# Leaving out the unused 512-column products behind six closing norms and ahead of the RWKV mixer

## What is computed

```python
for layer in range(DEPTH_2):
    g = norm_g[layer]
    h = h + 0.5 * rms_norm_2(swiglu(rms_norm_2(h, g[0]), ffn_w_in[layer, 0], ffn_w_out[layer, 0]), g[1])
    u = rms_norm_2(h, g[2])
    ...   # m = RWKV-7 time mixing (layer 0) or windowed attention (layer 1)
    h = h + rms_norm_2(m, g[3])
    h = h + 0.5 * rms_norm_2(swiglu(rms_norm_2(h, g[4]), ffn_w_in[layer, 1], ffn_w_out[layer, 1]), g[5])
```

## Time and profile before

| | us |
|---|---|
| median of 3 runs | 2985.78 |
| the three runs | 2983.85, 2985.78, 2999.92 |
| the profiled execution | 2985.55 |
| its span, first to last instruction | 2983.8 |
| PE busy in the span | 2887.4 |
| POOL, DVE, ACT busy | 1359.9, 954.4, 948.8 |

### The profile page before, as it was taken

One profiled execution on the slowest core, in us unless ns is written; L12 is line 12 of the kernel. 1 busy time (PEld: TensorE's weight loads), 2 busy tenths in 40 slices (PEclk: granted clock), 3 DMA queues, 4 the chain that ended last, 5 costly groups with the idle time before them and its releaser, 6 DMA issues.

```text
span 2983.8 us, 46814 instructions
## 1 busy us (share of the span) xinstructions
PE 2887.4 (97%) x19364; PEld 2347.7 (79%) x19364; DVE 954.4 (32%) x1455; ACT 948.8 (32%) x1104; POOL 1359.9 (46%) x1111
## 2 busy tenths in 40 slices
PE   8999999999999998898999999999999999999998
PEld 7768778888888886677887788887888877788887
DVE  3441332223312126435553412125211246321213
ACT  3243232222322225643342322224222236422222
POOL 5454444444444454333433444444444457544444
PEclk9999999999999999999999999999999999999999
DMA  5202222222222221441201222222222220122222
GB/s 194 91 21 93 99 85 90 94 99 99 85 99 99 99 99 57 183 167 42 66 30 65 85 95 91 97 101 92 91 98 99 99 88 30 71 85 97 90 96 85
DMA packets 43423, 271.64 MB, mean 91 GB/s; under 512 B 4832, under 2 KB 4960, under 8 KB 13824
## 3 DMA queue, kind: packets, MB, share of 16 engines
q1 hardware_dynamic: 40032, 252.64, 23.7%
q10 hardware_dynamic: 3232, 16.65, 1.4%
HBM read 254.59 MB, written 14.68 MB: 90 GB/s over the span
## 4 chain that ended last, share of the span: by engine, by line
issue 44%; POOL 31%; PE 22%; DVE 2%; POOLq 0%; DVEq 0%; ACT 0%; DMA 0%; SPq 0%; ACTq 0%
POOL w_lo L551 29%; PE ps L875 6%; PE ps L694 3%; PE ps L695 3%; PE ps L696 3%; POOL ybuf L626 1%; PE ps L828 1%; PE ps L783 1%; PE ps L860 1%; POOL x_res L662 0%; PE ps L847 0%; PE ps L760 0%; DVE work L1713 0%; DVEq L1710 0%; PE ps L794 0%
## 5 line engine op out<-in xcount | busy, mean ns | idle before, releaser
L551 POOL TENSOR_TENSOR w_lo<-w_raw,w_hi 128x512 fp32r<-128x512 f32 x876 | 1117.4, 1307 | 1358.8 <-ACT w_hi L1194 1358.8
L694 PE MATMUL ps<-act_hi,w_hi 128*128 128x512 f32 x2240 | 881.8, 394 | 27.9 <-DVE act_lo L1655 15.8
L695 PE MATMUL ps<-act_lo,w_hi 128*128 128x512 f32 x2240 | 877.2, 392 | 0.0
L696 PE MATMUL ps<-act_hi,w_lo 128*128 128x512 f32 x2240 | 876.6, 391 | 0.0
L1194 ACT CAST w_hi<-w_raw 128x2048 fp32r<-128x2048 f32 x219 | 418.0, 1909 | 1013.0 <-PE ps L696 985.7
L694 PEld LDWEIGHTS ps<-act_hi,w_hi 128*128 128x128 f32 x2240 | 423.5, 189 | 129.9 <-issue 21.8
L696 PEld LDWEIGHTS ps<-act_hi,w_lo 128*128 128x128 f32 x2240 | 423.5, 189 | 88.9
L695 PEld LDWEIGHTS ps<-act_lo,w_hi 128*128 128x128 f32 x2240 | 423.8, 189 | 86.6
L694 PE MATMUL ps<-hid_hi,w_hi 128*128 128x512 f32 x1184 | 463.7, 392 | 9.0 <-POOL w_lo L551 8.1
L696 PE MATMUL ps<-hid_hi,w_lo 128*128 128x512 f32 x1184 | 461.9, 390 | 0.0
L695 PE MATMUL ps<-hid_lo,w_hi 128*128 128x512 f32 x1120 | 436.9, 390 | 0.0
(11 more groups left out here) (262 smaller groups left out, 2341.3 us busy)
## 6 DMA issues: line engine op xcount, KB each, us to landing
w_raw<-stream SPq DMA_DIRECT2D x223, 1024.0 KB, 4.8
spill<-work ACTq DMA_DIRECT2D x3, 2048.0 KB, 8.4
scratch<-spill SPq DMA_DIRECT2D x24, 256.0 KB, 4.2
work<-bias_in SPq DMA_DIRECT2D x1, 3072.0 KB, 17.5
work<-spill SPq DMA_DIRECT2D x12, 256.0 KB, 3.3
x_res<-x_in SPq DMA_DIRECT2D x4, 512.0 KB, 7.0
spill<-work ACTq DMA_DIRECT2D x2, 1024.0 KB, 4.9
spill<-area ACTq DMA_DIRECT2D x1, 2048.0 KB, 10.8
```

Source lines behind the costliest of these rows:

```text
L551: inst = tt(w_lo[:, s, a:a + 512], w_raw[:, s, a:a + 512], w_hi[:, s, a:a + 512].bitcast(F32), ALU.subtract)
L694: mm(out, wh, hi[:, k, :], start=(k == 0) if begin is None else begin, stop=False)
L695: mm(out, wh, lo[:, k, :], start=False, stop=False)
L696: return mm(out, wl, hi[:, k, :], start=False, stop=end)
```

## The change

Both calls of stay_warm that stand behind a norm are removed: the one in `post_slabs` (six closing norms, four products each) and the one ahead of the RWKV mixer (four products). Nothing else is changed; no result depends on them.

```diff
@@ post_slabs
                 pe.wait_ge(S["sq_made"], 4 * NORM[name] + 4)
                 sum_of(name, 7, False, True).then_inc(S["sum_mm"], 1)
                 spread_rms(name)
-                stay_warm(4, bank=1 if name in AFTER_POST else 3)
@@ 
             ffn(0)
             sums("mixer0_pre")
             spread_rms("mixer0_pre")
-
-            stay_warm(4, bank=2)
 
             def mixed(j):
```

## The result

| | kernel before | changed kernel |
|---|---|---|
| median, us | 2990.81 (19 runs, the three shown among them) | 2999.05 (19 runs) |
| lowest and highest, us | 2981.88, 3002.76 | 2986.55, 3008.40 |
| ratio of the times | | 1.0033, 95% interval 1.0021 to 1.0044 |
| profiled execution, us (span) | 2985.55 (2983.8) | 2994.57 (2992.8) |

The change costs 8 to 10 us: 8.2 between the medians, 8.3 between the means, 9.9 by the ratio. That is within half a per cent, as forecast, and slower, as forecast; but the forecast was +3.4 us and 2989.0, with a range up to 2996.0, and the time lies 3 us outside. The other five are what has to be explained.

A forecast was written before the change was run, and what follows sets the result against it. PE was taken to bound the kernel, busy 97% of the span. Profiled execution 2985.55 us, plus 0 (removed products), 3.2 (four eager slabs) and 0.2 (before r), gave 2989.0 us, +0.1%; range 2983.5 to 2996.

The forecast's parts named there:

- Gain of the removed products: Behind six closing norms and before r: PE's busy time falls, but nothing waited for the products, so gain 0.
- The clock down at five restarts: Four eager slabs behind norms and the r slab would start at half clock, 1.2 GHz, without the products.
- Cold time of a restart: Each of the five restarts runs at half clock for 4.2 us (3.1 to 6.8), losing 2.0 us.
- Cover and price: At four eager slabs, waits for DVE hide 1.2 of 2.0 us; 0.8 us each is left, 3.2 in all.
- Rivals 1 to 3: Cover holds, 2985.6 us, 0.22; whole eager slabs at 1.2 GHz, 3002.8 us, 0.05; two half-clock stretches per restart, 2994.8 us, 0.10.
- rival 3: At each restart, two half-clock stretches, 6.8 us: 2994.8 us; chance 0.10 (+7 to +14 us).
- Rivals 4 and 5: Products held something up (PSUM writes or outlasting DVE's tile), 2981.6 us, 0.05; or the change doesn't remove them, excluded.
- Before r: At the r slab, waits after every tile cover a cold start of 2.0 us; 0.2 us taken as the cost.
- the stages behind shifted by the sum of these and by nothing else: Sign to look for: stages behind the slabs move only by the fifth tiles' delays, 0.3 to 2 us each.
- The base of the sum: The profiled execution, 2985.55 us, 0.23 under the median of 2985.78, to which the terms were added.

The follow-up runs named there:

- e1: Against the kernel before: products left out only behind the four norms that an eager slab follows (mixer0, ffn1, ffn2, mixer1); 2998.09 us, ratio 1.0021.
- e2: Against the kernel before: products left out only behind ffn0_post, ffn3_post and before r; 3001.65 us, ratio 1.0033.
- e3: The whole change once more, timed beside its two halves against the kernel before; 3003.14 us, ratio 1.0048.
- e4: Kernel before with six products instead of four behind the four norms that an eager slab follows; 2995.77 us, ratio 1.0009.
- e5: Kernel before with one-column products instead of 512-column ones behind ffn0_post, ffn3_post and before r; 2990.44 us, ratio 1.0001.
- e6: Kernel before with all 28 products of the change kept but cut from 512 columns to one; 2990.71 us, ratio 1.0004.
- e12: Changed kernel with 32 PE semaphore increments put in front of everything; 2999.98 us, ratio 1.0014 against the kernel before.
- e7 to e11: Kernel before with, in turn: twelve one-column products more behind ffn0_post; its four removed; 64, 128, 192 increments in front; 2997.11, 2992.91, 3000.68, 3008.02, 3023.76 us.

## Why the prediction was wrong, point by point

Lengths of three stages, from one profile each, between the same DVE operations (first normed input behind the norm ahead of the mixer; first operation of the scan; first term behind mixer0_post; first term behind ffn3_post), with the time at half clock in brackets:

| us | to the scan | scan and its output | rear |
|---|---|---|---|
| before | 155.53 | 352.18 (18.5) | 1321.92 (22.4) |
| changed kernel | 155.52 | 364.35 (33.8) | 1324.11 (48.2) |
| e1 | 155.44 | 358.33 (24.4) | 1325.99 (52.8) |
| e2 | 155.64 | 362.90 (29.2) | 1321.96 (24.9) |
| e3 | 156.21 | 362.01 (33.2) | 1324.12 (47.5) |
| e4 | 155.09 | 367.47 (43.2) | 1324.09 (23.6) |
| e5 | 156.76 | 359.70 (30.7) | 1321.46 (16.9) |
| e6 | 155.24 | 360.94 (33.6) | 1323.53 (46.9) |
| e12 | 156.33 | 366.89 (44.1) | 1323.31 (46.7) |

- **Gain of the removed products, forecast 0: right.** PE's busy time fell by 24.8 us (some 25 forecast at the end, some 30 where the products alone were counted) and nothing that the products stood beside became shorter. No sign was found that the products held anything up.
- **The clock down at five restarts: right**, in all kernels without the 512-column products, and at none of the four slabs behind norms in the kernels that keep them.
- **Cold time of a restart, forecast 4.2 us (3.1 to 6.8): right.** Over 20 restarts of the four eager slabs (the changed kernel, e1, e3, e6, e12) it was 4.4 on average, between 2.8 and 6.2; before r 3.1 to 5.6.
- **Cover and price, forecast 3.2 us for the four: right.** The rear stage is 1324.2 us in the five kernels with cold restarts against 1321.3 in the eight with warm ones and four products (before, e2, e5, e7 to e11): +2.9 us. Behind ffn1_post the slab's fifth tile was 1.3 us late where 0.8 was forecast. The timed runs agree but can't tell 3.2 from nothing (e6: -3.0 to +5.4). Rivals 1 to 3 fall with this as accounts of the restarts: the cover doesn't hold, no slab is cold throughout, and few restarts are as long as rival 3 has them all. Rivals 4 and 5 fall with the points above.
- **Before r, forecast 0.2: right within its scatter.** The stage is 155.95 us on average in the kernels with a cold r slab, 155.46 in the others.
- **"the stages behind shifted by the sum of these and by nothing else": this is the step that failed.** I had costed the removed instructions by what they do and when, and never by where they stand. The 32 instructions in front of the scan are worth some 7 us (4 to 10), put at nothing in the sum and about twice the whole forecast. In the two profiles too it is the stage that the change doesn't touch that became longer: the scan has +12.2, the rear +2.2, and what lies ahead of the mixer's normed input gives 5.3 back (1137.38 against 1142.72), for a span 9.0 longer. But single profiles don't show the place's effect there: in the six with the scan's code in its old place (before, e1, e4, e5, e6, e12) the scan takes 352.2 to 367.5 us, 360.9 on average, and in the three with 32 instructions less in front of it (the changed kernel, e2, e3) 362.0 to 364.4, 363.1 on average. The averages of the timed runs carry the argument. The rows had a hint: "issue" was the largest share of the chain, and I read it as PE working through its queue. A look at the waits of the scan's line would have shown 67 waits without a releaser.
- **The base of the sum** was a profiled execution of 2985.55 us and a median of three with 16 us between the lowest and the highest. Its scan, 352.2 us, is the shortest of the fourteen profiles. The range allowed a scatter of 1.9 us; nineteen runs moved the median by 5.0.

By the runs, then, the change is: cold restarts, +1.2 (-3.0 to +5.4) by e6 and +4.2 (+0.6 to +7.8) by e12, forecast +3.4; and the place of the code, some 7 (4 to 10). Together 7 to 13 with the forecast's 3.4, against +10 and +14 in the two comparisons.

Four things stay open. The packet of a long stop began late, but why it did at one border and not at the next wasn't tried. That the clock falls because of the stop before it is argued from the order of the two in the traces and from the averages, not shown by taking a stop away. That the loss arises in the scan is argued too: nearly all stops at the counted borders lie there, but the scan's length in the profiles scatters by more than the loss. And e12 was to bring the changed kernel down by the whole place effect; it moved all of PE's code, the scan's back to its old place and the rest's to a new one, and its interval (+0.6 to +7.8) allows both the forecast and some more.

## What to carry to other kernels

An instruction stream has a place as well as a cost: where an engine runs many short instructions, taking some away far in front of them moves them against the borders of their blocks. Here that went with 0.2 to 0.3% of the kernel's time, more than the work of the edit itself. So test such an edit beside a variant that keeps the count (one-column products here), before its mechanism is believed. And products that keep the clock up pay where the wait behind them is hidden only in part: here four of 512 columns fit it, one-column products don't keep the clock up, and six delay the slab (the rear stage of e4 is as long as with cold restarts, 1324.1 us, in one profile).

## What the runs showed of the hardware that was not expected

- PE stops for up to 2.2 us at multiples of 256 instructions (plus 149), some 10 to 18 times over 0.25 us in a stretch of 220 us with products of 64 x 64, and starts again 1.1 to 1.6 us behind the end of the last packet of the instruction queue. Stops of that length elsewhere in the stretch stand before semaphore instructions.
- The scan's length in fourteen profiles goes from 352 to 374 us, and follows the time at half clock in it (18 to 53 us; correlation 0.95, 0.57 us for each).
- Four products of one column behind each norm leave the clock at 1.2 GHz: e6's slabs start cold for 2.9 to 5.7 us, like those of the changed kernel.
- A semaphore increment on PE takes 0.15 us.
